# A hybrid decoder step on one core: the scan's chunks prepared one early, its group ends reworked, and the attention's loads queued in another order

## The chip, the cores and the metric

One core of a Trainium2 chip runs the whole program. The metric is the device time of one execution in microseconds (us). Engines: PE is TensorE (PEld its weight loads), DVE is VectorE, ACT is ScalarE, POOL is GpSimd, SP is SyncE, which issues all DMAs here.

## The reference, cut to what matters

A decoder trunk of two layers on 1024 prompt tokens and 8 sequences of 8 new tokens: one Mamba-2 (SSD) layer, then one layer of dilated window attention. The change is in the scan of the first and in the prompt part of the second.

```python
proj = u @ in_w                                  # z, x, B, C, dt
xbc = silu(causal_conv4(xbc))
acum = cumsum(dt * A)                            # inside a chunk of 128 tokens
cb = einsum('bclgn,bcsgn->bclsg', C, B)
y_diag = einsum('bclsgr,bcsgrp->bclgrp', cb * exp(acum_l - acum_s) (s <= l), x * dt)
states = einsum('bcsgn,bcsgrp->bcgrpn', B, x * dt * exp(acum_end - acum))
h = h * exp(acum_end) + states                   # from chunk to chunk
y = y_diag + (C @ h_in) * exp(acum) + x * D
y = rms_norm_by_group(y * silu(z)) @ out_w
```

Outputs are also the last states, the last conv rows and the K/V rows.

## The kernel before, in words

Everything is float32; a product with a large weight is three products of high and low parts. The program is written per engine (`sync`, `gpsimd`, `scalar`, `vector`, `tensor`), each with its own order by hand, joined by semaphores (`q`, `e`, `j3`, `f4`).

**First part (about 31 to 1031 us).** After the norm and the running sums of dt*A (L2299), a loop over four groups `g` of eight heads runs on every engine. In a group:
- *Columns*, L2313 to L2315: six tiles `f` of 128 columns (four of x, one of B, one of C), each 72 matmuls into three PSUM banks. ACT copies them to `raw` (L2080), DVE does the convolution (L2200 to L2209), ACT the silu (L2084). The weights of a tile come by DMA (L1910); ACT makes the high half (L2054), DVE the low half (L2180).
- *Chunks* `c` 0 to 7 (LC = 8) of 128 prompt tokens. On PE in order: x, B transposed (L2353, L2359), C by B (L2360), the segment sums as a product with a triangle (L2366, two products of 512 columns, for which POOL lays out `mix`, L1983), z (`multiply_z`, L2327 to L2329), the transposed y of the chunk before (`turn_y`, L2341), C by state (L2418), mix by xdt (L2422), B by xdtd for the new state (L2428). ACT evacuates x and B (L2100, L2106), takes one exp of 1024 columns (L2109), the silu of z (L2113), the transposed y (L2093), the square of y (L2127). DVE masks C by B into `cbm` (L2221), makes xdt (L2225), mix times cbm (L2229), four steps of y (L2248 to L2253), fades the state by `dec` (L2256), adds the new one (L2257), and normalises (L2259, L2261). POOL makes x times D in place (L1996), xdtd (L2003), the next chunk's `mix` (L1983) and the root (L2011).
- *Chunk 8* (64 tokens of the 8 sequences): DVE builds bseq, cseq, dexp (L2233 to L2237), PE spreads the decay (L2383), and then for each sequence turns the state (L2396), makes the new one (L2405) and the y of the old (L2411), while SP stores and loads states in four slots (L1940, L1920). Then L2422, the last state turned (L2432), y, and only then the next group's columns. After the loop the conv tails are turned (L2439) and stored (L1958, L1959), and all engines meet (L418).

**Middle (1031 to 1950 us)**: output projection, gate, K/V, q and gate projections, in tiles of which `rot` is stored on SP.

**Attention (from 1950 us)**: all engines meet; SP loads three masks (L1380); then 24 units `un` (3 dilations of 8 blocks). SP's order in a unit: q and k rows (L1427, L1428) once unit un-2 is turned; v rows (L1434, L1436) once `pv_done` of un-2; `store` of unit un-2 (L1389, L1390); in units 8, 9, 16 and 17 `load_queries` (twelve DMAs, L1401); in 22 and 23 `load_sequence` for the first sequences. PE turns k and q (L1735, L1739), scores (L1783), turns p (L1748), values (L1765).

Of the kernel before, what the change touches and what calls it, by code (L numbers as in the profile page):

```python
# [25 lines left out]
P = 128  # L26
# [5 lines left out]
D = 1024  # L32
# [98 lines left out]
def trunk_kernel(nc, a, o, s):  # L131

    outer = ExitStack()
    with outer:
# [92 lines left out]
        def con(name, rows=P):  # L227
# [25 lines left out]
        ea = sb("ea", [P, NT, NH])  # L253
        dend = sb("dend", [P, NT, NH])
# [3 lines left out]
        xt = sb("xt", [P, GW])  # L258
        btok = sb("btok", [P, DS])
        cbm = sb("cbm", [P, P])  # L260
# [9 lines left out]
        xdt = sb("xdt", [P, GW])  # L270
        xdtd = sb("xdtd", [P, GW])
        y = square[:, GW:2 * GW]
        zs = sb("zs", [P, GW])
# [5 lines left out]
        dexp = u[0:SAMP, 1, GW:2 * GW]  # L279

        st = raw[:, :, :].rearrange("p a w -> p (a w)")[:, 0:4 * XF * DS].rearrange("p (s f n) -> p s f n", s=4, f=XF)
        sdec = sb("sdec", [P, XF, NSEQ])
        tiny = xbc[:, 3:5, :].rearrange("p a b -> p (a b)")[:, 0:5 * NT * NH].rearrange("p (a b) -> p a b", a=5)
        dtT = xbc[:, CF - 1, :]

        cw_rows = xdt[0:(CK + 1) * CONVF, 0:P]
# [17 lines left out]
        _n = 2 + NG * IN_SPLITS  # L304
# [6 lines left out]
            x_full xt_ready bc_full btok_ready cbm_ready sum_ready seg_full e_ready m_ready z_full z_ready  # L311
# [4 lines left out]
        q = {n: sem(n) for n in names.split()}  # L316
        wx_landed = [sem(f"wx_landed{i}") for i in range(2)]
# [9 lines left out]
        VSTEPS = 2 + CF * (CK - 1) + 2 + NSEQ + 3 * NT + LC  # L327
# [88 lines left out]
        def meet(eng, k):  # L416
# [10 lines left out]
            added stored""".split()}  # L427
        wg_landed = [sem(f"wg_landed{j}") for j in range(2)]
# [116 lines left out]
        def stage2_sync(sp):  # L545
# [32 lines left out]
            def body(i, b, m, tb):  # L578
# [15 lines left out]
                for t in range(NT):  # L594
# [21 lines left out]
            sp.wait_ge(stored3[0], 16 * ((UNITS3 + 1) // 2))  # L616
            sp.wait_ge(stored3[1], 16 * (UNITS3 // 2))
            sp.wait_ge(j3["kv_out"], 16 * 2 * NGR)
            sp.wait_ge(e["stored"], 32)
# [340 lines left out]
        hp_landed = [sem(f"hp_landed{i}") for i in range(3)]  # L960
# [229 lines left out]
        def take_out(dve, t):  # L1190

            r = ROWS[t]
            dve.wait_ge(hp_landed[t % 3], 32 * (t // 3 + 1))
# [48 lines left out]
        def stage6_tensor(pe):  # L1242
# [27 lines left out]
            def turn_p(t):  # L1270
                r = ROWS[t]
                pe.wait_ge(hp_landed[t % 3], 32 * (t // 3 + 1))
# [103 lines left out]
        def section4_sync(sp):  # L1376
            meet(sp, 2)
            for tile, name in ((win, "win"), (pair, "pair"), (smask, "smask")):
                at, w = LAYOUT[name]
                sp.dma_start(tile[:, :], a["consts"][:, at:at + w]).then_inc(f4["m_landed"], 16)  # L1380
# [39 lines left out]
            def body(i, un, kind, before, nth):  # L1420
# [3 lines left out]
                alone(sp)  # L1424
                for hi in range(2):
                    ps = slice(64 * hi, 64 * hi + 64)
                    sp.dma_start(qn[ps, sl, :], rows4(s["q"][:, g, :], i, un, hi)).then_inc(qk_landed[sl], 16)  # L1427
                    sp.dma_start(kn[ps, sl, :], rows4(s["kv"][:, 0, g, :], i, un, hi)).then_inc(qk_landed[sl], 16)  # L1428
                if un > 1:
                    sp.wait_ge(f4["pv_done"], turn_of(i, 16, 8 * (un - 1)))  # L1430
# [9 lines left out]
                if un in EARLY:  # L1440
                    load_queries(EARLY.index(un))
                if un >= UN - 2:
                    load_sequence(None, un - (UN - 2), 0)
                    if un == UN - 1:
                        for d in range(2):
                            load_sequence(None, d, 1)

            units4(sp, body)
            store(None, UN - 2)
            store(None, UN - 1)  # L1450
# [32 lines left out]
            sp.wait_ge(ub_stored[1], 64 * (UN // 2))  # L1483
            load_merge(sp, 0)
            sequences(sp, sample)

        def section4_gpsimd(pool):
            meet(pool, 2)
# [29 lines left out]
        def section4_scalar(act):  # L1518
            meet(act, 2)
# [22 lines left out]

            act.wait_ge(f4["zeroed"], 2)
# [90 lines left out]
        def section4_vector(dve, chain):  # L1634
            meet(dve, 2)
# [88 lines left out]
        def section4_tensor(pe):  # L1724
            meet(pe, 2)
# [44 lines left out]
            for part in range(3):  # L1770
                turn(None, 0, part)

# [115 lines left out]
        def _(sp):  # L1888
# [13 lines left out]
            with sp.Fori(0, NG) as g:  # L1902
                for f in range(2, CF + 2):

                    n = f % CF
                    col = [(g + f // CF) * GW + XCOL + n * P, g * DS + BCOL, g * DS + CCOL][max(0, n - XF + 1)]

                    sp.wait_ge(q["xg_full"], g * CF + (f - 1))
                    alone(sp)
                    sp.dma_start(wx[:, f % 2, :, :], in_w[:, :, bass.ds(col, P)]).then_inc(wx_landed[f % 2], 16)  # L1910
                    if f == 2:
                        sp.wait_ge(q["z_full"], g * NT)
                        alone(sp)
                        sp.dma_start(wz[:, :, :], in_w[:, :, bass.ds(g * GW, GW)]).then_inc(q["wz_landed"], 16)
                        sp.wait_ge(q["yn_ready"], g * NT)
                        alone(sp)
                        sp.dma_start(nwg[:, :], a["m_norm_w"][:, bass.ds(g * GW, GW)].broadcast_to([P, GW])).then_inc(q["nw_landed"], 16)
# [17 lines left out]
                for c in range(LC):  # L1935
                    store_y(c)
                for n in range(NSEQ):
# [4 lines left out]
                    if n + 4 < NSEQ:  # L1942
                        sp.wait_ge(q["state_stored"], g * (16 * NSEQ) + 16 * (n + 1))
                        alone(sp)
                        load_state(n + 4)
                sp.wait_ge(q["fin_ready"], g + 1)
# [4 lines left out]
                             h0T[:, 0, :].rearrange("p (f n) -> p f n", f=XF)).then_inc(q["fin_stored"], 16)  # L1951
                store_y(LC)
            sp.wait_ge(q["yT_stored"], 16 * NT * NG)
# [529 lines left out]
```

## Time and profile before

| | |
|---|---|
| runs | 2753.75, 2755.72, 2759.09 us; median 2755.72 |
| profiled execution | 2756.31 us, of which 2754.5 us are the span of the trace |
| busy | PE 2511.3, DVE 1401.8, ACT 1045.6, POOL 398.1 us |
| mean granted TensorE clock | 0.95 of full |

The granted clock is a share of 2.4 GHz, and 0.50 is the lower level of 1.2 GHz. A row of the trace gives the start, the length (matmuls are pipelined and overlap, so their cost is read from start to start), the line, the operation with what it writes and reads, and in brackets the idle time of the engine before it and what ended that.

### The profile page before, as it was taken

What the parts mean: (1) busy time and instruction counts of PE and PEld (TensorE: products, weight loads), DVE (VectorE), ACT (ScalarE), POOL (GpSimd) and SP (SyncE); (2) the same over time, 40 slices, a digit from 0 to 9 for tenths busy, and PEclk for the clock granted to TensorE, in tenths of its full rate; (3) what the DMA queues carried; (4) which work ended last, traced back from release to release, by engine and by line L of the source; (5) the groups of instructions that cost most, each with busy time, mean ns of one, the idle gap of its engine ahead of it and who ended that gap; (6) DMA issues with size and microseconds to landing.
All of it is one profiled execution on the core that took longest, in us unless ns stands there. A gap on an engine that the chain in (4) does not pass through costs nothing.

```text
span 2754.5 us, 38441 instructions
## 1 busy us (share of the span) xinstructions
PE 2511.3 (91%) x12894; PEld 2054.1 (75%) x12894; DVE 1401.8 (51%) x3098; ACT 1045.6 (38%) x2179; POOL 398.1 (14%) x295
## 2 busy tenths in 40 slices
PE   4799799989989976999999999999798988998999
PEld 3787597687768745888778888888698887676776
DVE  3355365546536542333356287771376666248542
ACT  3235235324413432233242233331466767453321
POOL 0014104202400410000022043330100000001100
PEclk8899899889979998999999999999899999998999
DMA  3110221121031028332014423222333335875310
GB/s 107 50 50 20 60 81 31 58 76 39 24 102 47 23 66 278 84 92 95 31 50 151 148 79 110 74 78 78 85 76 78 90 92 121 245 186 180 129 55 20
DMA packets 228191, 243.60 MB, mean 88 GB/s; under 512 B 30711, under 2 KB 174959, under 8 KB 228040
## 3 DMA queue, kind: packets, MB, share of 16 engines
q1 hardware_dynamic: 228040, 241.60, 29.2%
q8 instruction: 93, 1.52, 0.2%
q14 instruction: 58, 0.48, 0.1%
HBM read 176.21 MB, written 69.14 MB: 89 GB/s over the span
## 4 chain that ended last, share of the span: by engine, by line
PE 65%; issue 17%; DVE 6%; POOL 5%; DMA 3%; ACT 2%; SPq 2%; POOLq 0%; DVEq 0%; ACTq 0%
PE bank L727 7%; PE bank L728 7%; PE bank L726 7%; PE bank L2313 4%; PE bank L2315 4%; PE bank L2314 4%; PE bank L1783 3%; PE bank L1765 3%; PE bank L651 2%; PE bank L652 2%; PE bank L653 2%; PE bank L1748 2%; POOL mix L1983 2%; PE bank L1838 2%; POOL xdtd L2003 2%
## 5 line engine op out<-in xcount | busy, mean ns | idle before, releaser
L726 PE MATMUL bank<-wh,uH 128*128 128x512 f32 x792 | 308.5, 389 | 0.0
L728 PE MATMUL bank<-wh,uL 128*128 128x512 f32 x792 | 308.1, 389 | 0.0
L727 PE MATMUL bank<-wl,uH 128*128 128x512 f32 x792 | 308.1, 389 | 0.0
L1563 ACT ACTIVATE sc<-sc,nmx 128x128 f32<-128x128 f32 (+1 forms) x384 | 169.7, 443 | 102.4 <-DVE nmx L1662 101.2
L2313 PE MATMUL bank<-uH,wxh 128*128 128x364 f32 (+1 forms) x576 | 193.9, 337 | 15.0 <-issue 10.0
L2315 PE MATMUL bank<-uH,wxl 128*128 128x364 f32 (+1 forms) x576 | 192.7, 334 | 5.7 <-issue 5.7
L2314 PE MATMUL bank<-uL,wxh 128*128 128x364 f32 (+1 forms) x576 | 193.0, 335 | 0.0
L726 PEld LDWEIGHTS bank<-wh,uH 128*128 128x128 f32 x792 | 148.7, 188 | 30.8
L728 PEld LDWEIGHTS bank<-wh,uL 128*128 128x128 f32 x792 | 148.7, 188 | 30.8
L727 PEld LDWEIGHTS bank<-wl,uH 128*128 128x128 f32 x792 | 148.7, 188 | 30.6
L1783 PE MATMUL bank<-kT,qT 128*128 128x128 f32 (+1 forms) x768 | 164.7, 339 | 1.3 <-ACT qT L1532 1.3
L1765 PE MATMUL bank<-vv,pT 128*128 128x64 f32 x1120 | 148.4, 268 | 0.1
L651 PE MATMUL bank<-woh,yh 128*128 128x512 f32 x288 | 114.1, 396 | 34.6 <-DVE wol L836 29.1
L639 POOL TENSOR_TENSOR hs<-hs,mhalf 128x8 f32<-128x8 f32 (+1 forms) x54 | 108.5, 2009 | 236.9 <-DVE hs L888 236.9
L1765 PEld LDWEIGHTS bank<-vv,pT 128*128 128x128 f32 x1120 | 141.9, 194 | 0.8 <-DVE pT L1642 0.3
L1658 DVE CUSTOM_DVE_ANT_0 sc<-bank,win 128x256 f32<-128x256 f32 (+1 forms) x256 | 87.8, 381 | 103.9 <-PE bank L1783 91.1
L2327 PE MATMUL bank<-wzh,uH 128*128 128x512 f32 x288 | 125.4, 436 | 6.1 <-ACT raw L2081 6.1
L1996 POOL TENSOR_TENSOR xt<-xt,vec 128x512 f32<-128x512 f32 (+1 forms) x36 | 67.2, 1867 | 429.6 <-DVE xdt L2225 429.6
L2313 PEld LDWEIGHTS bank<-uH,wxh 128*128 128x128 f32 x576 | 111.4, 193 | 21.9 <-issue 16.8
L1783 PEld LDWEIGHTS bank<-kT,qT 128*128 128x128 f32 x768 | 118.3, 197 | 6.6 <-ACT qT L1532 1.7
L1748 PE MATMUL bank<-cst,sc 128*128 128x128 f32 x560 | 96.8, 281 | 18.5 <-DVE pT L1642 18.2
L652 PE MATMUL bank<-wol,yh 128*128 128x512 f32 x288 | 113.0, 393 | 0.0
(337 smaller groups left out, 5527.6 us busy)
## 6 DMA issues: line engine op xcount, KB each, us to landing
yin<-scratch_yT SPq DMA_DIRECT2D x16, 1024.0 KB, 5.9
wr<-in_a_in_w SPq DMA_DIRECT2D x8, 2048.0 KB, 9.9
wx<-in_m_in_w SPq DMA_DIRECT2D x26, 512.0 KB, 3.9
scratch_q<-rot SPq DMA_DIRECT2D x48, 256.0 KB, 2.0
qn<-scratch_q SPq DMA_DIRECT2D x48, 256.0 KB, 3.6
scratch_u<-ub SPq DMA_DIRECT2D x48, 256.0 KB, 2.9
u<-scratch_u SPq DMA_DIRECT2D x24, 512.0 KB, 5.2
h<-in_x_prompt SPq DMA_DIRECT2D x2, 4096.0 KB, 19.4
```

The costliest lines, as they stand in the source:

```text
L651: pe.matmul(to, yh[:, v % 2, k, :], woh[j][:, k, :], start=(k == 0), stop=False)
L652: pe.matmul(to, yh[:, v % 2, k, :], wol[j][:, k, :], start=False, stop=False)
L726: pe.matmul(bank[:, t % 3, :], high, whigh, start=(k == 0), stop=False)
L727: pe.matmul(bank[:, t % 3, :], high, wlow, start=False, stop=False)
L728: last = pe.matmul(bank[:, t % 3, :], low, whigh, start=False, stop=(k == KT - 1))
L1563: last = act.activation(v, v, ACT.Exp, bias=nmx[:, sl, head(j, x):head(j, x) + 1], accum_out=mxs[:, sl, AH + head(j, x):AH + head(j, x) + 1])
L1748: last = pe.transpose(bank[:, 6, (x * kind + k) * P:(x * kind + k + 1) * P], sc[:, st0 % 4, 256 * x + k * P:256 * x + (k + 1) * P], ident)
L1765: last = pe.matmul(bank[:, 4 + hd // 8, (hd % 8) * HD:(hd % 8 + 1) * HD], pT4[:, st0 % 2, (x * kind + k) * P:(x * kind + k + 1) * P], vv[: ...
L1783: pe.matmul(bank[:, 2 * (st0 % 2) + x, 0:n], qT[:, sl, j, x, :], kT[:, sl, j // REP, 2 - kind:2, :].rearrange("p a n -> p (a n)"), start=T ...
L2313: pe.matmul(to, wxh[:, f % 2, k, :], uH[:, k, c0:c1], start=(k == 0), stop=False)
L2314: pe.matmul(to, wxh[:, f % 2, k, :], uL1[:, k, c0:c1], start=False, stop=False)
L2315: last = pe.matmul(to, wxl[:, f % 2, k, :], uH[:, k, c0:c1], start=False, stop=(k == KT - 1))
```

## The change

**Scan, chunks.** `xt`, `btok`, `cbm`, `xdt`, `y` and `zs` get two buffers. On PE chunk c+1's x, B, C products and z come ahead of chunk c's C by state; z of chunks 0 and 1 come first. The segment product (L2366) is gone: nine small products at the start transpose the running sums, ACT copies them negated, SP stores them to a scratch table (`acum`), and for every chunk SP loads the rows of eight heads into all partitions of `mix` (`load_decay`, a broadcast of 4 KB to 512 KB). DVE takes a maximum with the token's own negated sum (`bound_decay`), ACT makes eight exps with that as bias. mix times cbm goes from DVE to POOL, and so does the fade of the running state; POOL's root of a chunk comes behind the next chunk's mix.

```diff
-            def decay_sums(g, c, n):
...
+                    if c:
+                        pool.wait_ge(q["yd_full"], n)
+                        alone(pool)
+                        pool.tensor_tensor(hT.rearrange("p (h d) -> p h d", h=HG), hT.rearrange("p (h d) -> p h d", h=HG),
+                                           bc(dec[:, c - 1, bass.ds(g * HG, HG)], P, HG, HD), ALU.mult).then_inc(faded, 1)
                     pool.wait_ge(q["xdt_ready"], n + 1)
...
+                    mv = mix[0:r, c % 2, 0:HG * r].rearrange("p (h l) -> p h l", h=HG)
+                    pool.tensor_tensor(mv, mv, over(cbm[0:r, c % 2, 0:r], r, HG, r), ALU.mult).then_inc(q["m_ready"], 1)
+                    if c:
+                        root(n - 1, P)
```

```diff
+            def load_decay(g, c):
+
+                r = ROWS[c]
+                src = s["acum"][bass.ds(g, 1), c, :, 0:r]
+                sp.dma_start(mix[0:r, c % 2, 0:HG * r].rearrange("p (h l) -> p h l", h=HG),
+                             src.broadcast_to([r, HG, r])).then_inc(decay_landed[c % 2], 16)
...
                 for c in range(LC):
-                    store_y(c)
+                    if c + 2 < NT:
+                        sp.wait_ge(q["yd_full"], g * NT + c + 1)
+                        alone(sp)
+                        load_decay(g, c + 2)
+                    if c:
+                        store_y(c - 1)
+                store_y(LC - 1)
```

```diff
+            def bound_decay(g, c):
...
+                dve.tensor_tensor(v, v, bc(nacg[0:r, c, :], r, HG, r), ALU.max).then_inc(q["sum_ready"], 1)
...
+                def decay(c, n):
+                    r = ROWS[c]
+                    act.wait_ge(q["sum_ready"], n + 1)
+                    for hh in range(HG):
+                        v = mix[0:r, c % 2, hh * r:(hh + 1) * r]
+                        last = act.activation(v, v, ACT.Exp, scale=-1.0, bias=nacg[0:r, c, hh:hh + 1])
+                    last.then_inc(q["e_ready"], 1)
```

The order on DVE is now, for chunk c: `bound_decay(c+1)`, `spread(c+1)` (cbm, xdt), y of c, hT, the mean, then (behind POOL's root) the norm; in chunks 4 and 5 also the low halves of the next group's first two weights. ACT: z and x, B of c+1, `decay(c+1)`, (chunk 7: eight copies for bseq), in chunks 2 and 3 the high halves, transposed y of c-1, square of c.

**Scan, group ends.** In chunk 8 the first column tile of the next group is done in eight pieces between the sequences' products (`early_columns`), the state transposes alternate between two banks, y of chunk 7 is turned inside; then the last state is turned and the second column tile follows, ahead of the last y. The spreading product (L2383) goes to the start of the group. In the last group the tail transposes stand where the pieces stand in the others. The loop runs over three groups and the fourth is written out.

```diff
+            def early_columns(g, n, sq):
+
+                part = [(j, k) for j in (0, 2, 1) for k in range(KT)]
+                if sq == 0:
+                    pe.wait_ge(wl_ready, (g + 1) * IN_SPLITS + 2)
+                    pe.wait_ge(q["yT_ready"], n - 1)
+                    pe.wait_ge(q["z_ready"], n + 1)
+                    alone(pe)
+                for j, k in part[3 * sq:3 * sq + 3]:
...
+                            if end:
+                                if sq < CONVF // 4:
+                                    turn_tail(sq)
+                            elif sq + 2 < NSEQ:
+                                early_columns(g, n, sq + 2)
...
+                if not end:
+                    columns(g + 1, 1)
+                turn_y(LC, g * NT + LC)
```

**Attention.** The engines don't meet ahead of it. SP waits for the last projection product, loads q and k of unit 0, then the masks and the last gate store; in a unit, `load_queries` and the first `load_sequence` come behind q and k and ahead of the wait for `pv_done`.

```diff
-            meet(sp, 2)
...
+                if un == 0:
+                    sp.wait_ge(j3["full"], UNITS3)
                 for hi in range(2):
...
+                if un in EARLY:
+                    load_queries(EARLY.index(un))
+                if un >= UN - 2:
+                    load_sequence(None, un - (UN - 2), 0)
                 if un > 1:
                     sp.wait_ge(f4["pv_done"], turn_of(i, 16, 8 * (un - 1)))
...
-                if un in EARLY:
-                    load_queries(EARLY.index(un))
```

## Rows read from the trace of the kernel before

**Rows 1.** The page: busy time by engine, the chain that ended last, one costly group.
```profile
PE 2511.3 (91%) x12894; PEld 2054.1 (75%) x12894; DVE 1401.8 (51%) x3098; ACT 1045.6 (38%) x2179; POOL 398.1 (14%) x295
...
PE 65%; issue 17%; DVE 6%; POOL 5%; DMA 3%; ACT 2%; SPq 2%; POOLq 0%; DVEq 0%; ACTq 0%
...
L1563 ACT ACTIVATE sc<-sc,nmx 128x128 f32<-128x128 f32 (+1 forms) x384 | 169.7, 443 | 102.4 <-DVE nmx L1662 101.2
```

**Rows 2.** Windows: us; PE, PEld, DVE, ACT, POOL busy (count); granted clock; DMA share, GB/s.
```profile
441.00:514.00 73.00, 73.00 (x361) 54.45 (x361) 42.27 (x69) 37.70 (x56) 32.59 (x25) 1.00 0.08 22
520.00:537.00 17.00, 17.00 (x55) 10.35 (x55) 4.33 (x7) 2.34 (x4) 0.00 (x0) 0.52 0.23 73
579.00:640.00 61.00, 60.22 (x362) 59.92 (x361) 37.44 (x55) 20.73 (x38) 0.00 (x0) 1.00 0.27 82
987.00:1015.00 28.00, 23.71 (x136) 14.50 (x137) 11.22 (x17) 4.69 (x8) 0.00 (x0) 1.00 0.38 112
```

**Rows 3.** Timeline of PE around the start of the third group.
```profile
558.38 0.66 PE L2341 MATMUL bank<-cst,square 64*128 64x64 f32 x4 [6.53 <-DVE square L2261]
562.36 0.67 PE L2313 MATMUL bank<-uH,wxh 128*128 128x364 f32 x1 [3.32 <-issue]
...
565.25 0.46 PE L2315 MATMUL bank<-uH,wxl 128*128 128x364 f32 x1 [1.92 <-issue]
```

**Rows 4.** Timeline of PE ahead of the sequences, and at a first chunk.
```profile
519.07 1.15 PE L2383 MATMUL bank<-cst,u 64*128 64x8 f32 x5 [2.14 <-DVE u L2237]
...
653.09 1.10 PE L2418 MATMUL bank<-gain,xbc 128*128 128x512 f32 x2 [2.71 <-DVE mix L2229]
```

**Rows 5.** Timeline of PE in a chunk of the second group.
```profile
457.12 0.60 PE L2341 MATMUL bank<-cst,square 128*128 128x128 f32 x4
457.56 1.02 PE L2418 MATMUL bank<-gain,xbc 128*128 128x512 f32 x2
458.42 1.89 PE L2422 MATMUL bank<-xdt,mix 128*128 128x64 f32 x16
460.15 1.08 PE L2428 MATMUL bank<-xdtd,btok 128*128 128x512 f32 x2
...
461.83 1.88 PE L2366 MATMUL bank<-mix,cst 128*128 128x512 f32 x4
```

**Rows 6.** Groups of instructions, 441 to 514 us: busy us, mean ns, idle before.
```profile
L2109 ACT ACT_TABLE_LOAD x6 | 7.7, 1283 | 0.1
...
L2229 DVE TENSOR_TENSOR mix<-mix,cbm 128x1024 f32<-128x1024 f32 x6 | 7.4, 1226 | 1.0 <-ACT mix L2109 1.0
...
L2106 ACT COPY btok<-bank 128x128 f32<-128x128 f32 x5 | 1.3, 269 | 0.0
```

**Rows 7.** Timeline of POOL and DVE where both read SBUF.
```profile
428.74 1.04 POOL L1996 TENSOR_TENSOR xt<-xt,vec 128x512 f32<-128x512 f32 x1 [1.76 <-DVE xdt L2225]
...
428.99 1.87 DVE L2229 TENSOR_TENSOR mix<-mix,cbm 128x1024 f32<-128x1024 f32 x1 [0.43 <-ACT mix L2109]
...
429.74 2.03 POOL L2003 TENSOR_TENSOR xdtd<-xdt,dend 128x512 f32<-128x512 f32 x1
```

**Rows 8.** DMA issues: count, KB each, median us from issue to landing.
```profile
wx<-in_m_in_w SPq DMA_DIRECT2D x26, 512.0 KB, 3.9
...
gain<-in_m_norm_w SPq DMA_DIRECT2D x4, 256.0 KB, 10.1
...
gain<-in_norm_w SPq DMA_DIRECT2D x1, 512.0 KB, 15.2
```

**Rows 9.** Timeline of PE at the running sums.
```profile
86.64 3.97 PE L2299 MATMUL bank<-dta,cst 128*128 128x32 f32 x18 [12.35 <-DVE dta L2167]
```

**Rows 10.** Attention: PE's first instruction; PE's waits, 2000 to 2380 us; SP's issues.
```profile
1960.35 0.66 PE L1735 MATMUL bank<-cst,kn 128*128 128x128 f32 x2 [12.44 <-DMA kn<-scratch_kv]
...
PE bank L1735 <- DMA kn<-scratch_kv: 15.8, 5, 6.0
...
2100.53 4.48 SPq L1401 DMA_DIRECT2D uT<-scratch_q  x12
```

More of the change, by code:

```diff
@@ L2131, in _ @@
                 act.copy(h0T[:, 0, :], bank[:, 7, :]).then_inc(q["fin_ready"], 1)
[L2132 to L2135 removed]
+                if not end:
+                    head(g + 1)
+                    take_columns(g + 1, 0)
+                    take_columns(g + 1, 1)
+                turn(LC, g * NT + LC)
+            high_x(0, 0)
+            high_x(0, 1)
+            head(0)
+            take_columns(0, 0)
+            take_columns(0, 1)
+            with act.Fori(0, LAST) as g:
+                group(g, False)
+            group(LAST, True)
             stage2_scalar(act)
@@ L2260, in _ @@
                     dve.wait_ge(q["ry_ready"], m + 1)
-                    dve.scalar_tensor_tensor(y[0:r, :], y[0:r, :], ybuf[0:r, 2:3], nwg[0:r, :], ALU.mult, ALU.mult).then_inc(q["yn_ready"], 1)
-                chain.leave(NG)
+                    dve.scalar_tensor_tensor(yv, yv, ybuf[0:r, 2:3], nwg[0:r, :], ALU.mult, ALU.mult).then_inc(q["yn_ready"], 1)
+                    if c in (4, 5) and not end:
+                        low_x(g + 1, c - 4)
+                if not end:
+                    first(g + 1)
+                    convolve(g + 1, 0)
+                    convolve(g + 1, 1)
+            low_x(0, 0)
+            low_x(0, 1)
+            dve.wait_ge(q["cw_loaded"], 48 + 16 * NG)
+            dve.wait_ge(uT_full, NT)
+            chain(dve.memset(cseq[:, :, :], 0.0))
+            first(0)
+            convolve(0, 0)
+            convolve(0, 1)
+            with dve.Fori(0, LAST) as g:
+                chain.enter(g, VSTEPS)
+                group(g, False)
+                chain.leave(LAST)
+            group(LAST, True)
             stage2_vector(dve, chain)
@@ new lines, in turn_tail, with group @@
+            def turn_tail(j):
+                if j == 0:
+                    pe.wait_ge(q["yT_ready"], NG * NT - 2)
+                elif j == 1:
+                    pe.wait_ge(q["z_ready"], NG * NT)
+                else:
+                    pe.wait_ge(q["tail_ready"], j - 1)
+                for i in range(4):
+                    last = pe.transpose(bank[0:TAIL, 4 * (j % 2), i * P:(i + 1) * P], tail[:, 4 * j + i, :], ident)
+                last.then_inc(q["tail_full"], 1)
+            def group(g, end):
+                for f in range(2, CF):
+                    columns(g, f)
+                pe.wait_ge(q["raw_ready"], g * CF + CF - 1)
@@ L2433, in _ @@
                 last.then_inc(q["fin_full"], 1)
-                turn_y(NT - 1, g * NT + NT - 1)
-            for j in range(CONVF // 4):
-                if j > 1:
-                    pe.wait_ge(q["tail_ready"], j - 1)
-                for i in range(4):
-                    last = pe.transpose(bank[0:TAIL, 4 + j % 2, i * P:(i + 1) * P], tail[:, 4 * j + i, :], ident)
-                last.then_inc(q["tail_full"], 1)
+                if not end:
+                    columns(g + 1, 1)
+                turn_y(LC, g * NT + LC)
+            columns(0, 0)
+            columns(0, 1)
+            with pe.Fori(0, LAST) as g:
+                group(g, False)
+            group(LAST, True)
             stage2_tensor(pe)
```

588 lines of the change are left out of this document (343 added, 245 removed).

## The prediction

> **What bounds the kernel now.** TensorE is busy for 91% of the span and holds 65% of the chain that ended last [rows 1], so the first question is what TensorE does, and at which clock, in each stage. The windows table [rows 2] gives three kinds of stretch. In the scan over chunks (441 to 514 us) TensorE is busy for 73.00 of 73 us at full clock, and its 361 instructions at 59 a chunk make 6.12 chunks, 11.94 us each; nothing but less work on TensorE, or another engine becoming slower, can change this. In the column products (579 to 640 us) 362 of 72 a tile make 12.1 us a tile, also full. In the per-sequence part at a group's end (520 to 537 us) the clock stands at 0.52; this happened in three of the four groups, while the fourth ran it at 1.00 (987 to 1015 us). The timeline then shows the holes: 6.5, 3.3 and 1.9 us around the start of the next group [rows 3], 2.14 us before L2383 and 2.71 us before L2418 at the first chunk [rows 4]. This pattern repeats in every group. The rest of the program, after about 1031 us, is changed only where attention starts and in its queue.
>
> **Scan, a chunk.** From start to start the timeline of one chunk [rows 5] gives: L2341 0.44, L2418 0.86, L2422 1.73, L2428 with the transposes 1.68, L2366 1.88 less the overlap of 0.15 that the others show, so 1.73. The z product is the remainder, 5.5. The change drops L2366 (the decays now come from a scratch table by DMA, and are exponentiated with a bias), so TensorE's chunk becomes 10.2 us. What must fit under 10.2:
> - ScalarE: one exp of 1024 columns (1.03) becomes eight of 128. The nearest row is L2106, 0.27 for 128 columns [rows 6], so 2.2. With two table loads of 1.28 [rows 6], the z (0.60), two evacuations, one yT copy and the square it is some 7.6; at 0.44 an exp, the mean of L1563 [rows 1], 9. Covered either way, except once a group: the last chunk's yT copy stands behind the exps and eight new bseq copies (2.2), and TensorE's early column waits for it, about 2.7.
> - VectorE: the 1.23 product with cbm goes to GpSimd, a 1.23 maximum comes in its place, the fade (0.69) leaves. Left: four y steps at 0.72, hT 0.69, 0.15, yn 0.75, 1.23, 0.28, 0.68: 6.7.
> - GpSimd: decay sums (1.89) leave; fade (512 columns, 1.04), mix times cbm (1.89) come: 1.04 three times, 1.89, 0.54, so 5.6.
> The two are not independent. [Rows 7] show GpSimd's xt from 428.74 to 429.78, VectorE's mix beside it taking 1.87 for its usual 1.23 [rows 6], and GpSimd's xdtd then taking 2.03 for 1.04: each waits out the other. The Trainium skill, "SBUF — State Buffer", section "SBUF: two separate sides", calls the shared port pair an exclusive lock and names VectorE operations with two SBUF inputs as the ones that take it; by that rule the steps that read PSUM would not. The rows show the lock only for two SBUF inputs.
> I walk the loop, S being the first y step, 0.13 behind the end of L2422: GpSimd fades to S+1.06, takes xdtd when the state product is out, 1.4 to 2.4; the third y step waits for it, to 3.0; skip to 3.9; fourth y step to 4.45; mix to 6.2; root to 6.75; yn to 7.6; maximum, cbm, xdt to 9.55. VectorE is thus ready 0.65 before TensorE needs it again at 10.2, mix 2 us before. TensorE stays the bound. The low halves of the next weights (1.23) in chunks 4 and 5 eat the slack, about 1 us a group.
> - SP: one broadcast load of 512 KB a chunk, issued when L2422 is done and put ahead of the y stores, which only wait behind it for the issue. VectorE's maximum needs it 7.7 us later, and the next chunk's y steps are queued behind that maximum. The row of the same bytes in the same packets is wx, 3.9 us; the rows of the same kind (a broadcast) are gain's, 256 KB in 10.1 beside 2 MB of wz, and 512 KB in 15.2 at the program's start beside 4 MB of h [rows 8]. I take 4 to 5, hidden.
>
> **Scan, a group.** (a) Eight L2366 of 1.73 and a short one of 1.0: -14.8. (b) At the edge TensorE idled 11.8 us and ran the next column slowly (about 2 lost). Now column tile 1 follows the final transposes while VectorE finishes y, and tile 2 waits about 1.2 for its low half (fin copy, first convolution 5.9, subtraction 1.23 stand before it): -12.6. (c) The 2.14 idle goes with the moved L2383, the 2.7 of above comes: +0.6. (d) The 17 us at 0.52 cost 8.2. With column tile 0 filling in, 1.5 us beside 2.7 us a sequence, TensorE has no hole there: -8.2. (e) The first chunk now has z0 and z1 ahead, 0.7 between them for ScalarE, then about 5.0 idle while xt (0.6), btok (0.3), cbm and xdt (1.0) and GpSimd's three (4.0, and 0.7 for the lock) follow one another; before it was 1.5, 1.2 and 2.71: +0.3. Sum -34.7. A hole of 5 us may cost clock as 2.14 us did before; I put back 4 for (d) and 2 for (e): -29, for three groups -87. The last group has no tile to fill in and had full clock: (a), (c), (e), 3.7 of DMA waits covered by the 4.8 of tail transposes that now stand inside, 3 at the end because the conv outputs no longer follow the last y, 2 back for clock: -14.8 + 0.6 + 0.3 - 3.7 + 4.8 - 3 + 2 = -14.
>
> **Start.** Nine products for the transposed sums and three ScalarE copies stand before the first column. The sums of the same depth took 3.97 for nine chunks [rows 9] with 32 moving columns at half clock; with 128 I take 4.5, plus 1.6 of copies: +6. Bounds: 4 (all that lies beside the exps hidden) and 8.
>
> **Attention.** In 2000 to 2380 us TensorE waited 15.8 us for kn, the longest 6.0 [rows 10]. The twelve L1401 issues took 4.48 us of SP, and stood between the stores and the next unit's q and k; now they are issued behind the unit's own q and k, where SP waits for pv_done anyway: -15.8. V loads follow about a unit later and have that wait as cover; the cost if it is gone is 4.5. At the start TensorE idled 12.4 [rows 10]; three mask loads, the last gate store and the meeting leave the path, four issues of 0.5 and a landing stay: between 0 and -6.8, I take -4.5. Together -20.
>
> **Sum.** +6 - 87 - 14 - 20 = -115. The profiled execution took 2756.3 us (span 2754.5), 0.6 over the median of 2755.7; so 2641.
>
> **Rivals.**
> (B) Every VectorE step excludes GpSimd, PSUM readers too. For: no row shows a GpSimd operation running beside such a step. Then 6.5 of VectorE (without the 0.15) and 5.6 of GpSimd add up to 12.1 a chunk, 1.9 above 10.2, in 28 steps +53: 2694. The skill's rule named above speaks against it.
> (C) The clock stays low at the group ends. For: three groups of four fell after 2.14 us idle, and 2.7 and 5 us idle remain. Then (d) is not gained and the filled part loses as much again in half its length, some 12 more a group: 2677.
> (D) Slower: the broadcast load lands late. 128 partitions read the same 4 KB; the broadcast rows are 10.1 and 15.2. VectorE is in order, so a chunk is landing time plus 0.5 of issue plus 2.2 (maximum, cbm, xdt). It decides from 7.7 us on, cancels the whole gain at 11.6 us (chunk 14.3), and at 15.2 makes the chunk 17.9, +7.7 in 28 steps: +216, 2857. Against: both rows share their time with megabytes of other loads, and wx needs 3.9.
> (E) The change does less than it says: ScalarE or the low halves are late each group and the edge keeps its holes: +12.6 three times, 2679. For: two engines in order stand before tile 2.
> The Trainium skill's "GPSIMD Engine Reference", section 3.1, keeps elementwise work on VectorE as the rule, measuring GpSimd about twice slower. By it the fade is a loss on its own engine; the sum is unchanged as long as GpSimd has slack.
>
> **Chances.** Forecast 0.61, B 0.15, C 0.10, D 0.07, E 0.07. The low end is the sum without the 20 put back for clock, the four waits of 2.7 and 4 of the bounds on start and attention, 2606; the high end takes in B, C and E, 2700. A difference under 0.2% (5.5 us) can't be told from none. Faster 0.91, same 0.02, slower 0.07.
>
> **What would show it.** GpSimd's mix operation should repeat every 10.2 us; at 12 B holds; with VectorE's maximum waiting for a DMA, D. The landing of mix in the DMA view tells D at once, 4 to 5 against above 9. Clock above 0.95 in the group ends rules C out. TensorE should show no hole over 2 us between the final transposes and tile 2. Waits for kn should be gone. The prediction is wrong if the chunk isn't near 10.2, since that carries 48 of the 115.

## The result, and the profile after

The changed kernel takes **2648.0 us** (median of 4 runs, 2645.23 to 2651.64) where the kernel before took 2757.4 on the same chip (4 runs): ratio 0.9605, 95% interval 0.9586 to 0.9623, 109 us less. The forecast was 2641, within 2606 to 2700. One run of experiment 10 below, 3975 us at a granted clock of 0.57, is slow and left out of its numbers.

The page of the changed kernel, its parts 1, 4 and 6:

```profile
span 2648.0 us, 38588 instructions
...
PE 2436.3 (92%) x12776; PEld 2019.7 (76%) x12776; DVE 1424.3 (54%) x3033; ACT 1082.7 (41%) x2453; POOL 435.8 (16%) x327
...
PE 80%; DVE 7%; issue 4%; ACT 3%; DMA 3%; SPq 2%; POOL 1%; DVEq 0%; ACTq 0%; POOLq 0%
...
mix<-scratch_acum SPq DMA_DIRECT2D x32, 512.0 KB, 3.7
...
wx<-in_m_in_w SPq DMA_DIRECT2D x24, 512.0 KB, 4.0
```

TensorE lost 75 us of work, and the chain is now TensorE's for 80% where it was 65% [rows 1]: what went is work and idle time together. The broadcast load lands in 3.7 us.

The windows of the changed kernel, in the second group: chunks, sequences, column tile 1, tiles 2 to 5, and the first chunk.

```profile
439.00:475.00 36.00, 35.26 (x194) 28.16 (x193) 30.02 (x36) 27.32 (x59) 21.90 (x16) 1.00 0.21 68
491.00:526.00 35.00, 35.00 (x188) 25.98 (x187) 11.77 (x18) 5.86 (x11) 0.54 (x1) 0.95 0.33 98
528.00:540.00 12.00, 12.00 (x74) 12.00 (x75) 9.02 (x17) 4.09 (x14) 0.54 (x1) 1.00 0.30 86
543.00:590.00 47.00, 47.00 (x285) 47.00 (x284) 32.29 (x45) 22.59 (x44) 0.00 (x0) 1.00 0.37 116
406.00:416.00 10.00, 9.97 (x37) 8.11 (x38) 4.24 (x6) 0.72 (x2) 5.29 (x4) 0.68 0.17 54
```

The sequences, at 0.52 before [rows 2], run at 0.95 with TensorE never idle. But the second group was the worst. The whole part in the kernel before, in the first, second and third group:

```profile
287.00:317.00 30.00, 27.22 (x125) 15.64 (x126) 11.72 (x21) 4.69 (x8) 0.00 (x0) 0.84 0.35 105
519.00:550.00 31.00, 30.32 (x120) 18.23 (x120) 11.21 (x17) 4.69 (x8) 0.00 (x0) 0.72 0.33 101
750.00:781.00 31.00, 28.29 (x121) 16.43 (x121) 11.58 (x19) 4.69 (x8) 0.00 (x0) 0.80 0.34 102
```

As time times the missing share of the clock, that is 4.8, 8.7 and 6.2 us lost; the changed kernel has 0.94, 0.95 and 0.96 there (37, 36 and 36 us) and loses 2.2, 1.8 and 1.4. Clock is lost in another place: 0.68 in the ten microseconds behind the first chunk's hole.

The timeline of PE in the changed kernel shows the holes that are left in this group, and, last, one behind the scan:

```profile
406.03 3.22 PE L2633 MATMUL bank<-xdt,mix 128*128 128x64 f32 x14 [4.58 <-POOL mix L2055]
...
481.67 1.10 PE L2582 MATMUL bank<-gain,xbc 128*128 128x512 f32 x2 [1.34 <-DVE gain L2391]
...
490.84 0.53 PE L2492 MATMUL bank<-uH,wxh 128*128 128x364 f32 x1 [5.03 <-ACT yT L2156]
...
542.27 0.43 PE L2473 MATMUL bank<-uH,wxh 128*128 128x364 f32 x1 [1.38 <-DVE wxl L2290]
...
997.29 0.79 PE L657 MATMUL bank<-woh,yh 128*128 128x512 f32 x1 [4.33 <-DVE yl L837]
```

The first four repeat in the first three groups. The edge that had 6.5, 3.3 and 1.9 [rows 3] has the 1.4 before tile 2 alone.

One chunk in the timelines of DVE and of POOL (start, duration, and in brackets idle time with its releaser):

```profile
441.55 0.69 DVE L2381 TENSOR_TENSOR y<-bank,ea 128x512 f32<-128x512 f32 x1
442.27 0.69 DVE L2382 TENSOR_TENSOR y<-y,bank 128x512 f32<-128x512 f32 x1
443.00 1.37 DVE L2384 TENSOR_TENSOR y<-y,xt 128x512 f32<-128x512 f32 x1
444.40 1.42 DVE L2386 TENSOR_TENSOR y<-y,zs 128x512 f32<-128x512 f32 x1
...
448.62 0.75 DVE L2395 SCALAR_TENSOR_TENSOR y<-y,ybuf,gain 128x512 f32<-128x512 f32 x1 [1.85 <-POOL ybuf L2029]
449.28 1.22 DVE L2298 TENSOR_TENSOR mix<-mix,nacg 128x1024 f32<-128x1024 f32 x1
450.87 0.29 DVE L2344 TENSOR_TENSOR cbm<-bank,cst 128x128 f32<-128x128 f32 x1 [0.37 <-ACT btok L2168]
451.12 0.69 DVE L2348 TENSOR_TENSOR xdt<-xt,dtv 128x512 f32<-128x512 f32 x1
451.73 0.68 DVE L2381 TENSOR_TENSOR y<-bank,ea 128x512 f32<-128x512 f32 x1
```

```profile
441.46 1.08 POOL L2037 TENSOR_TENSOR gain<-gain,dec 128x512 f32<-128x512 f32 x1 [3.05 <-PE bank L2633]
442.78 1.05 POOL L2045 TENSOR_TENSOR xdtd<-xdt,dend 128x512 f32<-128x512 f32 x1 [0.24 <-PE bank L2642]
443.78 1.49 POOL L2049 TENSOR_TENSOR xt<-xt,vec 128x512 f32<-128x512 f32 x1
445.24 2.85 POOL L2055 TENSOR_TENSOR mix<-mix,cbm 128x1024 f32<-128x1024 f32 x1
448.05 0.53 POOL L2029 TENSOR_TENSOR ybuf<-ybuf,mhalf 128x1 f32<-128x1 f32 x1
```

The first y step stands at 441.55 and again at 451.73: 10.18 us, the forecast's 10.2. But it starts right behind the next chunk's xdt, 0.34 us after TensorE's product with mix ends; where VectorE waited for that product (second chunk, 421.12) it starts 0.27 after. So VectorE arrives about 0.1 us late, not 0.65 early. What slack it has stands at its third step, which waits for GpSimd's xdtd.

The 106.5 us between the spans, by the same places of PE's timeline: start +5.0; the first three groups, from one group's first product with mix to the next, 206.5, 205.4 and 204.7 for 231.4, 234.8 and 232.6, so 24.9, 29.3 and 27.9 less; the last group some 10 less. The first product of the output projection then comes 86.9 us earlier (966.41 for 1053.34), but its last only 83.6: the projection takes 3.3 us more, with a wait of 4.33 for yl where the kernel before had 3.06 and a clock of 0.84 for 0.93 over its first 40 us. The attention's first transposes come 90.3 us earlier than in [rows 10], so 6.7 are gained at its start (TensorE idles 5.75 there for 12.44), and the first sequence's result 106.6, so 16.3 in its units.

### The profile page after: what moved, and what is told of

Same layout as the page of the kernel before. It is cut to its first block, busy times and chain, and to the rows that moved or that the text cites. A ratio compares the mean times of both kernels' runs of the same rounds, so it can differ in the third digit from the quotient of the medians.

```text
span 2648.0 us, 38588 instructions
## 1 busy us (share of the span) xinstructions
PE 2436.3 (92%) x12776; PEld 2019.7 (76%) x12776; DVE 1424.3 (54%) x3033; ACT 1082.7 (41%) x2453; POOL 435.8 (16%) x327
## 4 chain that ended last, share of the span: by engine, by line
PE 80%; DVE 7%; issue 4%; ACT 3%; DMA 3%; SPq 2%; POOL 1%; DVEq 0%; ACTq 0%; POOLq 0%
PE bank L732 7%; PE bank L734 7%; PE bank L733 7%; PE bank L1795 3%; PE bank L1776 3%; PE bank L2473 3%; PE bank L2474 3%; PE bank L2475 3%; PE bank L657 2%; PE bank L658 2%; PE bank L659 2%; PE bank L2523 2%; PE bank L1759 2%; PE bank L2524 2%; PE bank L2525 2%
## 5 line engine op out<-in xcount | busy, mean ns | idle before, releaser
L2473 PE MATMUL bank<-uH,wxh 128*128 128x364 f32 (+1 forms) x504 | 167.1, 331 | 10.2 <-DVE wxl L2290 10.2
L2474 PE MATMUL bank<-uL,wxh 128*128 128x364 f32 (+1 forms) x504 | 166.4, 330 | 0.0
L2475 PE MATMUL bank<-uH,wxl 128*128 128x364 f32 (+1 forms) x504 | 166.2, 330 | 0.0
L809 ACT ACTIVATE raws<-bank,rstd 128x512 f32<-128x512 f32 (+1 forms) x54 | 37.1, 688 | 197.3 <-PE bank L734 171.9
L659 PE MATMUL bank<-woh,yl 128*128 128x512 f32 x288 | 114.1, 396 | 0.0
L2524 PE MATMUL bank<-wzl,uH 128*128 128x512 f32 x288 | 113.9, 395 | 0.0
```

What stands on the lines that cost most here:

```text
L2473: pe.matmul(to, wxh[:, f % 2, k, :], uH[:, k, c0:c1], start=(k == 0), stop=False)
L2474: pe.matmul(to, wxh[:, f % 2, k, :], uL1[:, k, c0:c1], start=False, stop=False)
L2475: last = pe.matmul(to, wxl[:, f % 2, k, :], uH[:, k, c0:c1], start=False, stop=(k == KT - 1))
```

## The experiments

Each is the changed kernel with the edit shown. "Plus" and "minus" are medians against 2648.0. Ratios are to the kernel before on the same chip: it took 2757.7 beside experiments 1 to 4 and 2753.2 to 2753.4 beside the others. By the ratios (the change itself has 0.9605) experiment 5 gives 17 us and not 21, and 6 costs 27 and not 23; 9 and 10 move by 3 to 4 and the others by 2 at most.

**1. The attention's queue order undone.**

```
-                if un in EARLY: load_queries(...)
-                if un >= UN - 2: load_sequence(None, ..., 0)
                 if un > 1:
                     sp.wait_ge(f4["pv_done"], ...)
                 ...
                     store(i, un - 2)
+                if un in EARLY: load_queries(...)
+                if un >= UN - 2: load_sequence(None, ..., 0); for the last unit part 1 too
```

> Only the attention's queue order is undone in the changed kernel: the loads for the merge step stand behind the stores again, ahead of the next unit's q and k. My theory (the twelve issues of 4.48 us held up q and k, and TensorE waited 15.8 us for kn): the waits for kn come back, about 3.7 us now against about 20 then, and the time goes from 2648 to 2664. Rival: the gain of 20 us in the attention came from its start (mask loads and the meeting left the path) and other transfers hid the queue: 2648 to 2650, waits for kn as they are now.

Measured: 2667.2, ratio 0.9673 (0.9657 to 0.969), plus 19. The waits for kn, attention's first transposes to its last unit, in the changed kernel and then in this one, each with PE's line at the start of the attention:

```profile
PE bank L1746 <- DMA kn<-scratch_kv: 9.4, 7, 5.7
...
1870.08 0.69 PE L1746 MATMUL bank<-cst,kn 128*128 128x128 f32 x2 [5.75 <-DMA kn<-scratch_kv]
```

```profile
PE bank L1748 <- DMA kn<-scratch_kv: 21.2, 7, 5.6
...
1869.58 0.69 PE L1748 MATMUL bank<-cst,kn 128*128 128x128 f32 x2 [5.59 <-DMA kn<-scratch_kv]
```

5.7 us of each is the start, so the units wait 3.7 us with the change and 15.6 without. The rival is out: the start is the same in both, and the whole 18 us lie in the units. The waits make 12 of them. In the windows of 50 us around them the granted clock is 0.93 (2000 to 2050) and 0.91 (2200 to 2250), where the changed kernel has 1.00: 50 by 0.07 and by 0.09 are up to 8 us more, so the clock can carry the other 6.

**2. The fade back on VectorE,** ahead of the first y step.

```
-                    if c: pool.wait_ge(q["yd_full"], n); pool.tensor_tensor(hT, hT, dec[c - 1], mult).then_inc(faded, 1)
+                    if c < LC: dve.tensor_tensor(hT, hT, dec[c], mult).then_inc(faded, 1)
```

> The fade of the running state goes back to VectorE, ahead of the first y step of the same chunk; the rest is the changed kernel. Theory L (the loop of VectorE and GpSimd runs over GpSimd's xdtd, which waits for the state product anyway, and VectorE's third y step waits for xdtd): 0.69 us more on VectorE disappears in that wait, chunk 10.2 to 10.3 us, time 2645 to 2652. Rival V (VectorE has only 0.1 us of slack a chunk, so each of its microseconds counts): chunk 10.8, in 32 chunks 19 us, 2667. Rival S (the fade is worse on GpSimd, which takes 1.08 for it, 0.69 on VectorE, and both exclude each other): the loop gets shorter, the chunks with a weight's low half gain up to 0.4 each, 2640 to 2645.

Measured: 2646.9, ratio 0.9605 (0.9589 to 0.9621), minus 1. The timeline of DVE in it:

```profile
440.77 0.68 DVE L2377 TENSOR_TENSOR gain<-gain,dec 128x512 f32<-128x512 f32 x1
441.38 0.68 DVE L2378 TENSOR_TENSOR y<-bank,ea 128x512 f32<-128x512 f32 x1
...
442.81 0.77 DVE L2381 TENSOR_TENSOR y<-y,xt 128x512 f32<-128x512 f32 x1
```

Theory L holds: the third y step, stretched to 1.37 by its wait for xdtd, now takes 0.77; the fade fills that wait. The chunk stays 10.18, so VectorE has 0.6 us of slack up to its third y step. The two chunks with a low half shrink from 11.15 and 11.79 to 10.56 and 11.29, which is a piece of S; the second chunk of the last three groups takes 0.6 to 0.9 more. Together the moved fade is worth nothing.

**3. The product of mix and cbm back on VectorE.**

```
-                    pool.tensor_tensor(mv, mv, over(cbm[...]), ALU.mult).then_inc(q["m_ready"], 1)
+                def weigh(c, m): (waits for e_ready and cbm_ready, then the same product on dve)
                 spread(0, g * NT)
+                weigh(0, g * NT)
                 spread(1, g * NT + 1)
+                weigh(1, g * NT + 1)
                 ... then_inc(q["msy_ready"], 1)
+                if 0 < c < LC: weigh(c + 1, m + 1)
```

> The product of mix and cbm goes back to VectorE (1.23 us there, 1.9 to 2.85 on GpSimd), behind the step that scales the square sum; for the first two chunks of a group it stands behind each cbm and xdt. Theory L (only steps with two SBUF inputs exclude GpSimd; what counts is the walk of both engines): VectorE and GpSimd are ready about 0.4 us before TensorE, the steady chunk stays 10.2, the two chunks with a low half lose 1.5 a group for 2.6, and the 4.6 us idle before the first chunk's y product become 1.5: 2630 to 2637. Rival V (VectorE's added 1.23 counts in full, since it has 0.1 of slack): chunk 11.3, 28 steps are 31 us, less 12 at the first chunks, 2667.

Measured: **2606.9**, ratio 0.9457 (0.9441 to 0.9474), minus 41; theory L had the direction and the mechanism, but expected only 11 to 18. The timeline of PE at its first chunk, and of DVE in a steady one:

```profile
392.20 1.97 PE L2639 MATMUL bank<-xdt,mix 128*128 128x64 f32 x16 [0.60 <-DVE mix L2350]
394.00 1.08 PE L2648 MATMUL bank<-xdtd,btok 128*128 128x512 f32 x2
```

```profile
429.79 1.22 DVE L2350 TENSOR_TENSOR mix<-mix,cbm 128x1024 f32<-128x1024 f32 x1
431.44 0.75 DVE L2401 SCALAR_TENSOR_TENSOR y<-y,ybuf,gain 128x512 f32<-128x512 f32 x1 [0.43 <-POOL ybuf L2029]
432.11 1.22 DVE L2293 TENSOR_TENSOR mix<-mix,nacg 128x1024 f32<-128x1024 f32 x1
433.97 0.29 DVE L2339 TENSOR_TENSOR cbm<-bank,cst 128x128 f32<-128x128 f32 x1 [0.64 <-ACT btok L2163]
434.22 0.69 DVE L2343 TENSOR_TENSOR xdt<-xt,dtv 128x512 f32<-128x512 f32 x1
434.83 0.68 DVE L2385 TENSOR_TENSOR y<-bank,ea 128x512 f32<-128x512 f32 x1
```

The added 1.22 goes into VectorE's 1.85 wait for the root. Its wait for btok grows to 0.64, slack that a low half can use: all chunks now take 10.2 (a group's last 10.4). In the second group, by PE's timeline: from the first product with the state to the first state product 3.4 us for 9.0; the next chunk 10.24 for 11.66; the two with a low half 2.4 less; the hole at the early column 4.37 for 5.03. That is 10.1 of the group's 10.6. Most is at the first chunk, 7.0 a group, of which the expectation had only the idle part.

**4. y's transposed copy ahead of the exps** in the last full chunk.

```
                         take_x(c + 1, n + 1)
+                        if c + 1 == LC: turn(c - 1, n - 1)
                         if c: decay(c + 1, n + 1)
                     ...
-                    if 0 < c < LC: turn(c - 1, n - 1)
+                    if 0 < c < LC - 1: turn(c - 1, n - 1)
```

> In the last full chunk of a group ScalarE copies y transposed ahead of the eight exps and the eight bseq copies, and not behind them. Theory (TensorE's 5.03 us hole before the early column is the wait for this copy, and the column then fills the time until the gate): the hole falls to about 0.5 us, the next wait is the one for VectorE's gate before the first state's transposes, under 1 us, and three groups give back 4.4 us each: 2635. Rival (what counts is bseq and the gate at the far end, which don't come earlier): the hole is only cut in pieces, before the transposes or the product with bseq, 2645 to 2650.

Measured: 2645.6 (2639.6 to 2649.43), ratio 0.9603 (0.9586 to 0.9621): as a time not told from the changed kernel. PE's hole at the first group's end in the trace:

```profile
286.45 0.63 PE L2597 MATMUL bank<-cst,raw 128*128 128x128 f32 x4 [1.87 <-issue]
```

The 5.03 before the early column is gone and 1.87 stands behind the column, before the first state's transposes, which by the program wait for VectorE's gate. The first three groups are 3.1 to 4.4 us shorter each, 11 together for the 13 of the theory, and the span of this profiled run is 2637.8. So the wait for the copy was real and goes. The gain in time isn't shown by this run alone: the median lies in the rival's range, the four runs fall into two pairs (2639.6 and 2642.1, 2649.2 and 2649.4), the trace is of the lowest, and what the other two lose is open.

**5. mix first on GpSimd in the first chunk,** ahead of xdtd and the skip.

```
+                    if not c: (the product of mix and cbm)
                     pool.wait_ge(q["xdt_ready"], n + 1)
                     ... (xdtd, skip)
-                    (the product of mix and cbm)
+                    if c: (the product of mix and cbm)
```

> The changed kernel, but in a group's first chunk GpSimd takes the product of mix and cbm ahead of xdtd and the skip, and not behind them. Theory F (most of the 41 us that the product on VectorE gave came from the first chunk: 5.6 us there and 1.4 in the second, through the 4.6 us hole and the half clock behind it, 28 in four groups; and what makes the hole is the order on GpSimd, not GpSimd's speed): the hole falls from 4.6 to about 1.5 us, the clock stays up, 5 to 6 us a group: 2624 to 2630. Rival (the steady loop's lack of slack is what costs, the product is simply 0.7 to 1.6 us longer on GpSimd and excludes VectorE in every chunk): the hole gets 2 to 3 us shorter and nothing else, 2636 to 2642.

Measured: 2626.8, ratio 0.9544 (0.952 to 0.9569), minus 21. Windows and PE's line at the first chunk:

```profile
400.00:410.00 10.00, 9.82 (x51) 7.89 (x52) 6.06 (x9) 1.99 (x6) 9.25 (x8) 1.00 0.18 54
...
400.18 1.97 PE L2640 MATMUL bank<-xdt,mix 128*128 128x64 f32 x16 [1.66 <-POOL mix L2044]
```

Theory F has the hole and the clock; the time is in its range, by the ratio 2 us above it (2632) and short of the rival's 2636. A hole of 4.58 put the next 10 us at 0.68; one of 1.66 leaves 1.00 here. But in the first group a hole of 1.65 is followed by 0.66 over ten us (197 to 207), and second chunks of 12.7 us there and 11.9 in the last group remain, so 1.66 is not safe. Two fifths to a half of what experiment 3 gave is thus a matter of order on one engine.

**6. The filling behind the sequences.**

```
-    early_columns(g, n, 0); early_columns(g, n, 1)     (ahead of the first state)
-    elif sq + 2 < NSEQ: early_columns(g, n, sq + 2)    (in each sequence)
+    for sq in range(NSEQ): early_columns(g, n, sq)     (behind the loop)
```

> The eight pieces of the next group's column tile 0 stand behind the eight sequences and no longer between them; the rest is the changed kernel. Theory (term (d): the filling keeps the clock up, and costs no time of its own): TensorE has holes in the sequences, its clock falls there to about half as before the change, a group is 8 us longer, three groups 25: 2672. Rival (the filling only moves 12.1 us of columns to where TensorE would have run them anyway, since TensorE's own part of a sequence is 4.17 less 1.5, 2.7 us, and the clock stays up without it): 2646 to 2652, clock near 1.0 in the part.

Measured: 2670.8, ratio 0.9703 (0.9673 to 0.9733), plus 23; by the state products a group takes 214.8 us on average for 205.6. Windows of the same part, 10 us each:

```profile
499.00:509.00 10.00, 9.90 (x35) 6.88 (x35) 4.26 (x7) 1.89 (x4) 0.54 (x1) 0.50 0.09 26
509.00:519.00 10.00, 8.01 (x32) 3.66 (x32) 2.76 (x4) 2.25 (x4) 0.00 (x0) 0.84 0.39 114
519.00:529.00 10.00, 9.65 (x42) 5.76 (x42) 4.08 (x6) 1.55 (x3) 0.00 (x0) 0.76 0.59 174
```

By the clock this is 9.0 us lost (10 by 0.50, 0.16 and 0.24), where the changed kernel loses 1.8 (35 by 0.05); a new wait of 2.0 for a state's load makes the rest. The filling keeps the clock up, and that is what it is worth in the changed kernel. It is not the same as what was lost before: here the part stands behind a hole of 5.22 us, in the kernel before behind one of 2.14.

**7. The broadcast load issued at the gate,** 4.3 us later.

```
-                        sp.wait_ge(q["yd_full"], g * NT + c + 1)
+                        sp.wait_ge(q["gated"], g * NT + c + 1)
```

> In the changed kernel the broadcast load of a chunk's decays is issued when y is gated instead of when the y product is out, 4.3 us later; it then lands about 8.5 us behind the y product, where VectorE reaches the maximum at 7.8. Theory (the maximum stands in VectorE's queue ahead of the next y steps, and VectorE has 0.1 us of slack): a wait for a DMA of about 0.7 us before each maximum, chunk 10.9, in 28 chunks 20 us: 2668. Rival (there are several us of cover left behind the maximum, since only the exps need it): chunk 10.2, 2648.

Measured: 2666.3, ratio 0.9675 (0.9647 to 0.9702), plus 18. The timeline of DVE in a chunk of the third group, and in one of the first:

```profile
645.36 1.23 DVE L2298 TENSOR_TENSOR mix<-mix,nacg 128x1024 f32<-128x1024 f32 x1 [0.73 <-DMA mix<-scratch_acum]
...
237.81 1.48 DVE L2298 TENSOR_TENSOR mix<-mix,nacg 128x1024 f32<-128x1024 f32 x1 [2.12 <-DMA mix<-scratch_acum]
```

The 0.7 is there, but that chunk still takes 10.18: the 0.6 found by experiment 2 takes it up, and the last group keeps its 10.2 throughout. In the first two groups, from the fourth chunk on, waits of 0.9 to 2.1 stand before the maximum and the chunks take 10.9 to 13.4. The gate that releases the next load comes later by each delay, which would explain it; that is not shown by itself. So the sum came near by a mechanism that the expectation didn't have. As the change has it, the load is some 3.6 us early.

**8. Experiments 3 and 4 together.**

> Both edits together: the product of mix and cbm on VectorE, and y's transposed copy ahead of the exps in the last full chunk. If the two gains come from different places (41 us from first chunks and chunks with a low half; 3 to 4 us a group from the hole at the early column): 2607 less 11 is 2596. Rival (with VectorE faster at the gate the hole was already shorter, 4.37 for 5.03, and the exps moved back now hold up VectorE's product in its queue): 2602 to 2607.

Measured: 2599.0, ratio 0.9435 (0.941 to 0.946), minus 49. PE's hole in the second group:

```profile
468.85 1.13 PE L2619 MATMUL bank<-u,xdtd 64*128 64x128 f32 x8 [1.63 <-ACT u L2201]
```

Between the theory (2596) and the rival (2602 to 2607): 8 us under experiment 3, 6 by the ratios, whose intervals overlap. In the traces the first three groups are together 5.3 us shorter than in experiment 3, where the moved copy alone gave 11: half of it adds up. The wait that is left is for the bseq copies, behind eight exps on ScalarE.

**9. These two, and the fade on VectorE too.**

> As the kernel with both edits, and the fade on VectorE too, ahead of the first y step, so that GpSimd keeps only xdtd, the skip and the root. Theory L (the fade hides in VectorE's wait for xdtd, so the engine that does it makes no difference to a chunk): the same as with both edits, within 4 us, steady chunk 10.2. Rival V (VectorE has 0.64 us of slack a chunk now, and the fade is 0.69 on it; a low half of 1.22 comes on top in two chunks): two chunks a group 0.7 longer and more, 4 to 8 us slower than with both edits. Rival S (the fade is cheaper on VectorE and leaves the exclusion): 3 us faster.

Measured: 2601.5, ratio 0.945 (0.9421 to 0.9479), not told from 2599.0; the chunks take 10.2. L again; V's loss in the chunks with a low half isn't there, nor is S's gain.

**10. As experiment 8, with the ninth chunk's exps and product moved** between the sequences.

```
-                        if c: decay(c + 1, n + 1)
+                        if c and c + 1 < LC: decay(c + 1, n + 1)
                             if sq == 2:
+                                decay(LC, n)                      (ScalarE)
-                    if 0 < c < LC: weigh(c + 1, m + 1)
+                    if 0 < c < LC - 1: weigh(c + 1, m + 1)
+                            if sq == 2: weigh(LC, m)              (VectorE)
```

> The kernel with both edits, and the ninth chunk's exps no longer ahead of the eight bseq copies but behind the second sequence's state copy on ScalarE, with VectorE's product for that chunk behind the third sequence's state update. Theory (the 1.63 us hole before the product with bseq is the wait for these copies, and the square of the eighth chunk, 2.3 us late for VectorE, stands behind them too): no hole before the product with bseq, clock up through the sequences, 1.6 to 2.5 us a group: 2590 to 2594. Rival (the gate before the first state's transposes, or the third sequence, which now waits for ScalarE's 3.3 us of exps, takes the wait over): 2597 to 2602.

Measured: **2590.5** (2590.4 to 2595.8, three runs), ratio 0.9406 (0.9379 to 0.9432), minus 58 and 163 less than the kernel before on the same chip. At the place where the changed kernel idled for 5.03 PE's timeline has

```profile
460.48 0.40 PE L2503 MATMUL bank<-uH,wxh 128*128 128x364 f32 x1 [0.19 <-issue]
```

and no hole over 0.8 us follows until the next group's tile 2, which waits 0.7 to 1.4. The theory holds. It is the fastest version tried, and it keeps the change's structure.

## Why the prediction was right

The time came out 7 us above the forecast, and the chunk, which carries most of it, came out as said. That the total is so near is partly luck: against the forecast's terms the groups gave 9 us less (82 and 10 for 87 and 14) and the output projection, held to be unchanged, lost 3, while start and attention gave 4 more. By its own steps:

- **The chunk** (term a): 10.18 where 10.2 was forecast, in every chunk without extra work. In the walk of the loop GpSimd's mix ends 6.5 behind the first y step for 6.2, the root 7.0 for 6.75, yn 7.8 for 7.6, and maximum, cbm and xdt take 2.4 for 1.95, with a wait of 0.37 for btok between them that the walk had not: 10.2 for 9.55. So nothing was left of the slack of 0.65 at the first y step; the 0.6 that experiment 2 found stands at the third.
- **Chunks 4 and 5:** mis-sized, 2.6 us a group for about 1, by that slack. A low half takes VectorE 1.22 and makes the one chunk 1.0 longer and the other 1.6.
- **The edge** (b): right in its mechanism; tile 2 waits 1.1 to 1.4, forecast 1.2. But the 11.8 us of holes at one edge were taken for all three, and the other two had 10.0 and 11.0.
- **The hole at the early column** (c): mis-sized, 5.0 for 2.7. The eight exps (2.0) and eight bseq copies (2.4) were counted; two table loads of 1.28, the silu of z (0.59) and the copies of the ninth chunk's x and btok in front of them were not: ScalarE reaches the copy at 489.9, having started at 481.7. Experiment 4 takes this wait away.
- **The clock in the sequences** (d): right in its mechanism, by experiment 6, where undoing the filling costs 9.3 a group, 7 of it clock. Its size was misread. The 17 us at 0.52 stood in the second group alone; by the windows above the three groups lost 19.7 us and not 24.6, and now lose 5.4. That is 14 gained, near the 12.6 that the sum had with its 4 a group put back. Rival C, the low clock staying, is out for this part (0.94 to 0.96; the forecast's own sign was above 0.95). In the last group, without filling, the same part stands at 0.79 (897 to 930).
- **The first chunk** (e): its hole was right, 4.6 for 5.0. The clock behind it cost 3.2 in the second group for the 2 put back (1.5 in the second chunk, 1.7 on the product with mix), but the kernel before paid for clock here too, with second chunks of 13.9, 14.5 and 14.3 us for 11.9 in three groups, which the sum left out. The hole was accepted as given; experiments 3 and 5 show that a choice of the change makes it, GpSimd's product behind two other steps.
- **Three groups:** 82 for 87. The two mis-sized terms come to 3.9 a group, 12 for three; the 6 a group put back for clock were more than needed and cover the rest. **The last group** gave about 10 for 14: it has a wait of 3.4 us before the first state's transposes, with no early column to hide behind, and one of 1.7 for a state's load, and the clock falls behind them. **The start** cost 5.0 for 6.
- **The output projection:** not in the sum, which took the program from about 1031 us to the attention as unchanged; it lost 3.3.
- **The attention:** 23 for 20, 6.7 at its start for 4.5 (the far bound was 6.8) and 16.3 in the units for 15.8. Experiment 1 shows the queue as the cause in the units, and adds what the sum didn't have: its waits of 12 us cost some 18, with the clock. That the units' term came out is partly luck: it took the waits for kn to vanish whole, where 3.7 us remained, and had no clock.
- **Rival B** is out: VectorE's first two y steps, which read PSUM, take 0.69 beside GpSimd's fade at 1.08, and only the steps with two SBUF inputs are stretched (1.37 and 1.42). This agrees with the Trainium skill, "SBUF — State Buffer", section "SBUF: two separate sides".
- **Rival D** is out: 3.7 us. That the broadcast rows of [rows 8] were slow for what ran beside them is likely by this, not shown. Experiment 7 shows that its rule, VectorE held up by a late load, is real, and that 4.3 us later it decides.
- **Rival E** came true in one place only: ScalarE is late at the early column, the edge is clean.

The forecast called the fade's cost hidden, and experiments 2 and 9 agree. It gave the product with cbm on GpSimd no price but its place in the walk, and looked at the first chunk only for what it added to the old idle time (+0.3). GpSimd is idle for 3 us in a steady chunk and still holds up TensorE in the first one, and VectorE in all of them. The rule of the Trainium skill, "GPSIMD Engine Reference", section 3.1, to keep elementwise work on VectorE, was right for the product (41 us) and made no difference for the fade.

## What to carry to other kernels

Work given to an engine with idle time is free only if no one waits for it: walk the first pass of a loop, where the pipeline is empty, as well as the steady one, and put first what the bottleneck waits for. Two engines that take turns at the same memory must be added up step by step, for the steps that exclude each other. A hole on TensorE costs its length and then clock behind it: here 3 us more after 4.6 (0.68 over ten), 1.8 after 5.0 with the filling behind it, and 9 after 5.2 without it. So fill or split holes ahead of saving work elsewhere.

## What was not expected of the hardware

- A VectorE step with two SBUF inputs waits for the whole GpSimd instruction that is running: the gate step, 0.69 alone, took 2.75, ending behind GpSimd's mix product. The lines of both in the changed kernel's timelines:

```profile
478.17 2.75 DVE L2386 TENSOR_TENSOR y<-y,zs 128x512 f32<-128x512 f32 x1
...
477.55 2.83 POOL L2055 TENSOR_TENSOR mix<-mix,cbm 128x1024 f32<-128x1024 f32 x1
```

- The other way, GpSimd's root over one column, 0.53 alone, took 1.47 beside VectorE's 1.22 product in experiment 3.
- After a hole of 4.58 us the granted clock was 0.68 over the next ten; after one of 1.66 it was 1.00 in the second group, and 0.66 after one of 1.65 in the first. In the attention of experiment 1, waits of 4.2 to 4.7 us brought stretches of 50 us down to 0.91 to 0.96.
- A load in which 128 partitions read the same 4 KB, 512 KB in all, landed in 3.7 us, as fast as one with different rows (wx, 4.0).
